# Inputs of a two-layer decoder trunk laid out in DRAM as the loads read them, and a reordered head

## The reference

```python
y = jax.nn.gelu(x @ w_y + b_y, approximate=True)
u = x @ w_x + b_x
upad = jnp.concatenate([conv_buf, u], axis=1)
xc = conv_b + sum(conv_w[k] * upad[:, k:k + T] for k in range(CONV_W))
r = sigmoid(einsum('btni,nij->btnj', xb, w_ga) + b_ga)
gi = sigmoid(einsum('btni,nij->btnj', xb, w_gi) + b_gi)
log_a = -LRU_C * r * softplus(-lam)
a = exp(log_a); bterm = sqrt(-expm1(2 * log_a)) * (gi * xc)
h = associative_scan(a1 * a2, a2 * b1 + b2)      # over time
x = layer_norm(ALPHA * x + (h * y) @ w_out + b_out)
x = layer_norm(ALPHA * x + square(relu(x @ w_up)) @ w_down)
```

## Time and profile before

| | |
|---|---|
| median of 3 runs | 1062.01 us (1061.81, 1062.01, 1064.13) |
| profiled execution, first to last instruction | 1061.3 us |
| TensorE busy with matmuls | 1045.2 us (98%) |
| VectorE / ScalarE / GpSimd busy | 840.5 (79%) / 662.7 (62%) / 226.3 us (21%) |
| DMA, mean over the span | 131 GB/s |
| mean granted TensorE clock | 0.994 of full |

### The profile page before, as it was taken

The page is one execution under the profiler, slowest core; times in us unless marked ns, Lnnn a source line. Parts: engine busy times, 40 slices in busy tenths (PEclk is TensorE's granted clock), DMA queues, the critical chain, the costliest instruction groups (busy, mean ns, idle before and its releaser), DMA issues.

```text
span 1061.3 us, 21612 instructions
## 1 busy us (share of the span) xinstructions
PE 1045.2 (98%) x8247; PEld 1022.6 (96%) x8247; DVE 840.5 (79%) x1289; ACT 662.7 (62%) x1159; POOL 226.3 (21%) x285
## 2 busy tenths in 40 slices
PE   8999999999999999999999999999999999999996
PEld 8999999999999999999999878999999999999995
DVE  6999898989779697696974674888879697696885
ACT  5999858665736547463666775675836647457432
POOL 2111032011111111103234564210111111111023
PEclk9999999999999999999999999999999999999998
DMA  7323214468877877865141211164777877878402
GB/s 255 120 90 100 79 61 141 99 158 159 177 164 158 196 159 157 200 163 197 32 128 46 62 62 40 40 179 81 159 167 163 194 156 155 201 159 177 136 11 75
DMA packets 54460, 139.54 MB, mean 131 GB/s; under 512 B 5632, under 2 KB 21440, under 8 KB 54368
## 3 DMA queue, kind: packets, MB, share of 16 engines
q0 software_dynamic: 14512, 53.60, 29.7%
q1 hardware_dynamic: 39584, 84.32, 24.3%
q10 hardware_dynamic: 288, 0.59, 0.2%
HBM read 135.95 MB, written 3.56 MB: 131 GB/s over the span
## 4 chain that ended last, share of the span: by engine, by line
PE 92%; DVE 2%; ACT 2%; issue 1%; POOL 1%; DMA 1%; SPq 0%; DVEq 0%; POOLq 0%; ACTq 0%
PE bank L2493 8%; PE bank L2474 8%; PE bank L2495 8%; PE bank L2219 8%; PE bank L2494 8%; PE bank L2475 8%; PE bank L2476 8%; PE bank L2220 8%; PE bank L2221 8%; PE bank L2306 3%; PE bank L2307 3%; PE bank L2308 3%; PE bank L2614 1%; PE bank L2588 1%; PE bank L2447 1%
## 5 line engine op out<-in xcount | busy, mean ns | idle before, releaser
L832 ACT ACTIVATE w_hi<-stage 128x1024 fp32r<-128x1024 f32 x164 | 168.3, 1053 | 128.9 <-DMA stage<-w_up 74.1
L1352 DVE TENSOR_TENSOR w_lo<-stage,w_hi 128x1024 fp32r<-128x1024 f32 x164 | 197.0, 1219 | 57.8 <-ACT w_hi L832 57.7
L2493 PE MATMUL bank<-part_hi,w_hi 128*128 128x288 f32 (+1 forms) x672 | 195.5, 291 | 0.0
L2495 PE MATMUL bank<-part_hi,w_lo 128*128 128x288 f32 (+1 forms) x672 | 194.9, 290 | 0.0
L2494 PE MATMUL bank<-part_lo,w_hi 128*128 128x288 f32 (+1 forms) x672 | 194.3, 289 | 0.0
L2219 PE MATMUL bank<-x_hi,w_hi 128*128 128x288 f32 (+1 forms) x496 | 145.2, 293 | 1.0 <-issue 1.0
L2220 PE MATMUL bank<-x_lo,w_hi 128*128 128x288 f32 (+1 forms) x496 | 143.7, 290 | 0.0
L2221 PE MATMUL bank<-x_hi,w_lo 128*128 128x288 f32 (+1 forms) x496 | 143.1, 288 | 0.0
L2493 PEld LDWEIGHTS bank<-part_hi,w_hi 128*128 128x128 f32 x672 | 127.2, 189 | 1.8 <-issue 1.8
L2494 PEld LDWEIGHTS bank<-part_lo,w_hi 128*128 128x128 f32 x672 | 127.5, 190 | 0.0
L2495 PEld LDWEIGHTS bank<-part_hi,w_lo 128*128 128x128 f32 x672 | 127.3, 189 | 0.0
(11 more groups left out here) (295 smaller groups left out, 2913.4 us busy)
## 6 DMA issues: line engine op xcount, KB each, us to landing
stage<-w_up SPq DMA_DIRECT2D x54, 512.0 KB, 3.7
stage<-w_down SPq DMA_DIRECT2D x52, 512.0 KB, 4.2
stage<-w_down POOLq DMA_DIRECT2D x48, 512.0 KB, 5.6
stage<-w_up POOLq DMA_DIRECT2D x44, 512.0 KB, 5.7
stage<-w_qkv SPq DMA_DIRECT2D x10, 512.0 KB, 4.1
stage<-w_x SPq DMA_DIRECT2D x8, 512.0 KB, 5.4
stage<-w_y SPq DMA_DIRECT2D x8, 512.0 KB, 3.5
stage<-w_out SPq DMA_DIRECT2D x8, 512.0 KB, 3.7
```

Of the source, the lines that this page charges most:

```text
L832: A(w_hi[:, slot_of(l, k), :], raw_of(l, c, k), ACT.Copy).then_inc(s_whi, 1)
L1352: vt.tensor_tensor(w_lo[:, s, :], raw_of(l, c, k), w_hi[:, s, :].bitcast(F32), ALU.subtract)\
L2493: mm(out, wh, xh[:, k, :], start=(fresh and k == 0), stop=False, skip_group_check=True)
L2495: ins = mm(out, wl, xh[:, k, :], start=False, stop=(k == 1), skip_group_check=True)
```

## The change

It stores x, the `w_x` and `w_y` slabs, the gates, `w_out`, `w_qkv` and `w_o` in DRAM so that each partition's share of a transfer is one run there (2 KB for x and gates, 4 KB for slabs); splits slab 0 and slab 1 into halves of two k, each half loaded and split right behind the x piece that it is multiplied with; loads both parts of the vectors from SP, the first behind the four slabs, the second behind the gates; loads x for h = 1 in four pieces; takes y(0) and x(1) k by k too; sets `WARM` to 9; moves `derive_in` and `derive_series` behind `x_split(1)` on VectorE, and the exp behind it on ScalarE. The arithmetic is the same.

```diff
-WARM = 13
+WARM = 9
@@ SP
-            load_x(0)
-            load(0, xv[:, 0:4, 0:256])
-            for k in (1, 2):
-                load_x(k)
-            load(1, xv[:, 4:8, 0:256])
-            load_x(3)
-            load_pair(("pair", 0), yv, 0, 2)
+            def load_x(k):
+                sp.dma_start(acc[:, 2 * k:2 * k + 2, 0:256], x_a[k].rearrange("p (k t) -> p k t", k=2))\
...
+            def load_front(j):
+                sp.dma_start(stage[:, where[j][0], 0:512], w_in[j][:, 0:512]).then_inc(s_front[j], 16)
+
+            def load_back(j):
+                sp.dma_start(stage[:, where[j][0], 512:1024], w_in[j][:, 512:1024]).then_inc(s_arrived[where[j][0]], 16)
+
+            late = VEC["sinks"][0]
+            for j in range(2):
+                load_x(2 * j)
+                load_front(j)
+                load_x(2 * j + 1)
+                load_back(j)
+            load_slabs(("pair", 0), w_in, 2, 2, 2)
+            sp.dma_start(vecs[:, 0:late], vec[:, 0:late]).then_inc(s_vec, 16)
             for p in range(4):
                 if p == 0:
-                    sp.dma_start(acc[:, :, 256:512],
-                                 xp_t[:, 256:512].rearrange("(k p) t -> p k t", p=128)).then_inc(s_xb, 16)
-                    sp.dma_start(acc[:, :, 512:TOK], xs_t.rearrange("(k p) t -> p k t", p=128)).then_inc(s_xb, 16)
+                    for k in range(4):
+                        load_x_rest(k)
                 else:
...
+                load(job_at[("gates", p)][0], w_gates[p])
+                if p == 0:
+                    sp.dma_start(vecs[:, late:NVEC], vec[:, late:NVEC]).then_inc(s_veclate, 16)
@@ ScalarE
-            x_split(0, [0])
-            late = VEC["sinks"][0]
-            act.dma_start(vecs[:, 0:late], vec[:, 0:late]).then_inc(s_vec, 16)
-            split([0])
-            x_split(0, [1, 2])
-            split([1])
-            x_split(0, [3])
+            for j in range(2):
+                x_split(0, [2 * j])
+                front(j)
+                x_split(0, [2 * j + 1])
+                back(j)
             split([2, 3])
             act.wait_ge(s_vec, 16)
-            act.dma_start(vecs[:, late:NVEC], vec[:, late:NVEC]).then_inc(s_vec, 16)
@@ ScalarE, step s
                 act.wait_ge(s_halo, s + 1)
-                if s == 0:
-                    act.wait_ge(s_sp, 1)
-                    A(tiny[:, 2, :], tiny[:, 1, :], ACT.Exp, scale=-1.0).then_inc(s_spe, 1)
                 copy_u(s, 0)
...
                 if s == 0:
                     x_split(1)
+                    act.wait_ge(s_sp, 1)
+                    A(tiny[:, 2, :], tiny[:, 1, :], ACT.Exp, scale=-1.0).then_inc(s_spe, 1)
@@ VectorE
             halo(0)
+            x_split(1)
             dve.wait_ge(s_vec, 16)
             derive_in()
             derive_series()
             for s in range(8):
...
-                if s == 0:
-                    x_split(1)
-                else:
+                if s:
@@ TensorE
+                    group_by_k(range(2), 0, pair_pieces(w0),
+                               lambda k: ((s_xlo, k // 2 + 1), (s_wlo if k % 4 > 1 else s_frontlo, k // 4 + 1)))
+                    group_by_k(range(mark[("y", 0)], mark[("y", 0)] + 2), 0, pair_pieces(w0 + 2),
+                               lambda k: ((s_wlo, j + 3 + k // 4),))
```

More of the change, by code:

```diff
@@ L227, in sem @@
             return ctx.enter_context(nc.semaphore(name))
-        s_vec = sem("vec_loaded")
+        s_vec, s_veclate = sem("vec_loaded"), sem("late_vec_loaded")
         s_xa = [sem(f"x_half_a_loaded_{k}") for k in range(4)]
-        s_xb = sem("x_half_b_loaded")
+        s_xb = [sem(f"x_half_b_loaded_{k}") for k in range(4)]
+        s_front = [sem(f"front_of_slab_loaded_{j}") for j in range(2)]
+        s_fronthi, s_frontlo = sem("front_hi_done"), sem("front_lo_done")
         s_arrived = [sem(f"slab_arrived_{i}") for i in range(STAGES)]
@@ L673, in load, with load_slabs @@
                 put(where[j][0], src)
[L675 to L681, removed]
+            def load_slabs(name, w, first, n, jj=0):
+                for k in range(n):
+                    load(job_at[name][0] + jj + k, w[first + k])
             def bring(l, c, k, on, src, after):
@@ L752, in _ @@
-                    sp.dma_start(acc[:, :, 512:TOK], xs_t.rearrange("(k p) t -> p k t", p=128)).then_inc(s_xb, 16)
-                else:
[L754 to L762, removed]
+                    for k in range(4):
+                        load_x_rest(k)
+                else:
+                    load_slabs(("pair", p), w_in, 4 * p, 4)
@@ L1415, in _, with front, back @@
             vt.memset(tiny[:, 7, :], 0.0).then_inc(s_hlo, 2)
-            x_split(0, [0])
-            split([0])
-            x_split(0, [1, 2])
-            split([1])
-            x_split(0, [3])
+            def front(j):
+                hi, lo, raw = split_targets(j)
+                dve.wait_ge(s_fronthi, j + 1)
+                vt.tensor_tensor(lo[:, 0:512], raw[:, 0:512], hi[:, 0:512].bitcast(F32), ALU.subtract)\
+                    .then_inc(s_frontlo, 1)
+            def back(j):
+                hi, lo, raw = split_targets(j)
+                dve.wait_ge(s_whi, j + 1)
+                vt.tensor_tensor(lo[:, 512:1024], raw[:, 512:1024], hi[:, 512:1024].bitcast(F32), ALU.subtract)\
+                    .then_inc(s_wlo, 1)
+            for j in range(2):
+                x_split(0, [2 * j])
+                front(j)
+                x_split(0, [2 * j + 1])
+                back(j)
             split([2, 3])
```

72 lines of the change are left out of this document (42 added, 30 removed).

## The result

| | before | after |
|---|---|---|
| median | 1062.49 us (21 runs) | 1064.42 us (21 runs) |
| lowest to highest | 1061.26 to 1064.13 us | 1063.69 to 1065.36 us |
| ratio of the two | | 1.0015, interval 1.0009 to 1.0021 |
| profiled execution: span, time | 1061.3 us, not known | 1062.8 us, 1064.75 us |

The change makes the kernel 1.9 us (0.15%) slower. That is under the 0.2% that I had called telling, but over the forecast of 1062.3 and beyond its range (1058.8 to 1063.2).

What follows compares the result with a forecast made beforehand. The VectorE and ScalarE relay, started by the first convolution, was taken to set the end. Gains 0.85 (slab) and 0.81 (copies) less 1.92 (series) gave -0.26 us, so 1062.01 + 0.26 = about 1062.3 us, range 1058.8 to 1063.2.

Steps and rivals of the forecast that it cites:

- The other engines' relay: Recurrent stage: VectorE and ScalarE run at their own pace from the first convolution, so only its start moves the end.
- rival 2: Recurrent stage: VectorE and ScalarE have room, TensorE sets the end; 2.4 to 3.4 us gained, 1058.6 to 1059.6; chance 0.17.
- The series' price of 1.92 on the relay: Before the first convolution: derive_in, exp and derive_series, moved behind x_split(1), add 1.92 us with nothing to hide them.
- the three new kinds of waits: TensorE waits for the gate input of steps 0 to 5, m_lo, and longer for the sum of squares: 2.7 us.
- SP's queue put at 0: Head loads: ten issues of about 0.5 us ahead of the vectors, against eight, cost 0; 256 KB per issue outpaces the queue.
- Longer runs, 0.26 us: Loads of the four slabs: longer DRAM runs move faster, landing the last slab 0.26 us earlier; lower end 0.
- Rival 4: Slab loads: the longer runs bring nothing; 1062.5 us; chance 0.05.
- Vectors behind the slabs, 0.59 us: Head loads: 213 KB less ahead of the last slab lands it 0.59 us earlier.
- rival 1: Head loads: one share's lag vanishes or halves, last slab 1.1 to 2.2 us earlier; 1060.1 to 1061.2; chance 0.22.
- The copies' release, 0.81 us: ScalarE's copies of x(0) out of PSUM no longer wait for TensorE, which held them up by 0.81 us.
- `WARM` 9 put at nothing: TensorE's head: the shorter warm-up, ending at 5.05 us, lies on no path and costs nothing.
- Rival 3: TensorE's head: the clock drops, all x(0) may run at 1.2 GHz, ending at 18.4; 1065.3 us; chance 0.08.

Runs made afterwards that it cites:

- E2: The kernel before with only the softplus series (derive_in, derive_series) moved behind the split of x for h = 1: 1064.70 us, ratio to before 1.0017.
- E3: The kernel after with slabs 0 and 1 loaded whole, still split in halves: 1063.43 us, ratio to before 1.0007.
- E10: E1 with the four half slabs issued by ScalarE instead of SP, so the same transfers on two queues: 1062.56 us, ratio to before 0.9997.
- E7: The kernel after with the head of before (load order, whole slabs, splits, vectors on ScalarE's queue, series first, 13 warm-up matmuls): 1062.01 us, ratio to before 0.9988.
- E6: The kernel after with slabs 0 and 1 loaded whole and the series first again: 1062.12 us, ratio to before 0.9992.
- second and third profile of before: The unchanged kernel before profiled twice more: 1063.35 us (later group of its times) and 1062.36 us (earlier group).
- E9: The kernel after with whole slabs 0 and 1, lam loaded first, all of softplus(lam) between VectorE's first splits, halo(0) ahead of them: 1062.60 us.
- E13: The kernel after with 13 warm-up matmuls instead of 9: 1063.85 us, ratio to before 1.0010.
- E14: E6 with 13 warm-up matmuls instead of 9: 1061.61 us, ratio to before 0.9986.
- E1: The kernel after with the series ahead of the split of x for h = 1 again and ScalarE's exp ahead of its copies: 1062.96 us, ratio to before 1.0003.
- E8: E6 with halo(0) ahead of VectorE's splits and the exp behind the copies of x(0): 1062.18 us, ratio to before 0.9989.
- E4: The kernel after with the four halves of slabs 0 and 1 each packed contiguously in DRAM: 1063.94 us, ratio to before 1.0010.

## Why the prediction was wrong

- **What held.** The other engines' relay sets the time, and not TensorE: rival 2 is refuted by E2 (TensorE's head untouched, 1064.70) and by the table. The series' price of 1.92 on the relay was 1.89. x(0) was to start at 5.7 and started at 6.07 to 6.4. Its idle time, the cover of x for h = 1, and two of the three new kinds of waits came as written.
- **The failed step: SP's queue put at 0.** "256 KB in 0.5 us is more than the queue drains" compared bytes issued with bytes moved. That comparison holds in the trace (1.3 MB issued at 3.9 us, 0.5 MB moved), and it was the wrong test: the queue moved less, though bytes stood in it. The issues take 0.6 us, and E3 and E10 show that eight transfers of 256 KB on one queue cost 0.9 us (thirteenth share 13.03 against 12.12) up to 1.4 (split at 13.54 against 12.11). I had priced halves as a gain only.
- **Longer runs, 0.26 us: net 0** (E7). The gain was there, 0.2 us for each `w_y` slab, more than forecast. What the term left out is that the new layout makes the first pieces later, in E7 by 0.4 us at the first x piece. E7 is one profile, so both are good to 0.2 us or so. Rival 4 has the net right and not the reason.
- **Vectors behind the slabs, 0.59 us: measured 0.7** (E6 against E7), within the scatter of 0.5 to 1.0.
- So the last slab's share came 0 + 0.7 - 0.9 = -0.2 us, later instead of 0.85 earlier; measured directly it is 0.3 to 0.6 later (12.95 and 13.03 against 12.43 to 12.68). That the low part was ready 0.26 sooner than in rows 4 all the same is the lag that had gone (rival 1's mechanism, without its time).
- **The profile I started from.** I took the part around the span, 0.7 us, from the median and the profiled span. In the second and third profile of before, and in E2, E7 and E9, it is 2.15 to 2.2 us, and in each of the other executions of before 2.1 to 2.2. The profiled execution thus took about 1063.5 and was of the later group. The median to which I added was of the earlier one, in which the convolution starts at 20.30 and the copies wait for VectorE and the exp (16.12), not for TensorE. A profile and a time of different executions had been put into one sum.
- **The copies' release, 0.81 us: 0.5 to 0.7, and the wait was misread.** TensorE held the copies up by 0.20 us only, as rows 3 say in their brackets; the rest was the exp, which stood ahead of them and waited for its input from VectorE:

```profile
16.59 0.21 ACT L931 ACTIVATE tiny<-tiny 128x8 f32<-128x8 f32 x1 [1.65 <-DVE tiny L1427]
```

From the low part to the copies it is 0.81 us here, 0.50 and 0.59 in the second and third profile, where they don't wait for TensorE at all, and 0.11 in after. The size was nearly right because the change moved the exp too.
- **`WARM` 9 put at nothing** was right for the head. For the program it was 0.5 to 0.6 us in the two pairs E13 and E14, 950 us further on, though other kernels with 9 don't have that loss.

The sum, from the third profile of before (1062.36) to the profiled execution of after (1064.75): convolution 22.28 - 20.30 = 1.98; from there to the squares 0; from the squares to the end 911.90 - 911.22 = 0.68; around the span 1.91 instead of 2.17, -0.26. Together 2.4, as measured (2.39). The first term taken apart: the last slab's low part is ready at 15.93 instead of 15.53 (+0.40), the copies start 0.11 behind it instead of 0.59 (-0.48), from them to x's last low part it is 4.42 instead of 4.26 (+0.16), and the convolution stands 1.82 behind that instead of 0.08 ahead (+1.90, the series). Against the forecast's -0.85, -0.81, 0 and +1.92 the first of these misses by 1.25 us, over half of the 2.1 us between forecast and result, and SP's queue is 0.9 of it; the end of the program, put at nothing, adds 0.7.

**Rivals.** Rival 1 came in part: the last slab's lag is 0.42 us in after, where rows 3's slab had 1.32. Rival 3 (clock) did not come: the granted clock is 1.00 in every stretch of after's head, TensorE's longest pause there being 1.5 us. What stays open: why the wait in the last MLP comes and goes. It went with the four matmuls in both pairs, but E1 and E8 to E10 have 9 matmuls and all but lack it too, so the place of the instructions is not all of it. Also open: what in SP's one queue is slow, and why the new layout starts later. Nor do the runs show why the part around the span is 1.9 us in most kernels of the new order and 2.15 to 2.2 in the others (before, E2, E7, E9).

## What to carry to other kernels

Cutting a first load in two so that work can start sooner pays only as long as the queue keeps the engines fed: read the GB/s of the first stretches, and put the halves on a second queue before giving them up. Before costing a head, ask which engine's first link sets the end, and price each moved instruction by whether that link waits for it. A term that measures 0 can be two that cancel: read the steps in between (here the distance of two landings) before calling it absent. And match a profile to the time of the same execution: if the times fall into groups, know which group the profile is of.

## What the runs showed of the hardware

- Eight transfers of 256 KB issued by one engine every 0.6 us: 245 GB/s from 4 to 8 us (225 to 261 in five profiles of such kernels); six, two of them 512 KB: 338 GB/s; eight from two engines: 340 GB/s. Mostly pieces of 288 KB from one queue, from 14 to 18 us: 406 GB/s.
- Slabs of 512 KB in runs of 1 KB landed 1.49 to 1.50 us apart (350 GB/s), in one run of 4 KB per partition 1.27 to 1.33 us apart (about 400 GB/s). SP's first seven issues took 0.44 to 0.51 us each in the first layout and 0.54 to 0.69 in the second (E7).
- The last share or two of a transfer's 16 can land 1.7 to 2.1 us behind the thirteenth in one execution and 0.3 us behind it in the next of the same kernel. In three profiles of before it went with a first convolution 0.9 us later.
- TensorE lost 0.4 to 1.2 us near 972 us, for nothing that the profile shows, in four kernels with 9 warm-up matmuls (after, E3, E4, E6), at most 0.2 in four others with 9, and nothing in those with 13 (before, E2, E7, E13, E14).
- The granted clock was 0.58 of full from 8 to 12 us in E8, behind a pause of TensorE of 3.0 us (4.99 to 8.00), the lower level of 1.2 GHz for most of it. The copies waited for that x(0). Behind pauses of 2.45 (E9) and 2.49 us (E7) it was 0.61 from 8 to 12 us. In the same place of the kernel before it fell behind 2.08 us in the first profile (0.83 from 12 to 14 us) and stayed at 1.00 behind 2.34 us in the second, so the length of the pause alone does not tell.
